# Loading the two halves of an expert weight matrix in one DMA of 2 MB into two neighbouring ring slots

## The reference, cut to what matters

```python
def moe_swiglu(x, w_router, w_gate, w_up, w_down):
    logits = (xt @ w_router).astype(jnp.float32)
    top_val, top_idx = lax.top_k(logits, TOP_K)              # 2 of 8
    top_w = jax.nn.softmax(top_val, axis=-1)
    gates = jnp.sum(jax.nn.one_hot(top_idx, N_EXPERTS) * top_w[..., None], axis=1)
    for e in range(N_EXPERTS):
        y = y + gates[:, e:e + 1] * swiglu(xt, w_gate[e], w_up[e], w_down[e])
```

## Time and profile before

| | us |
|---|---|
| runs | 1366.14, 1364.48, 1365.83 |
| median of the runs | 1365.83 |
| span of the profiled execution, first to last instruction | 1365.5 |
| expert stage, from the profile (first expert gate work to last down) | about 478 to 1350 |

### The profile page before, as it was taken

How to read it: one execution, slowest core, us unless ns; L and a number is a source line. 1 busy time by engine, 2 the same in 40 slices (tenths; PEclk the granted TensorE clock), 3 DMA queues, 4 the chain that set the end, 5 groups by cost and what they waited for, 6 DMA issues and landing times.

```text
span 1365.5 us, 18288 instructions
## 1 busy us (share of the span) xinstructions
PE 1331.8 (98%) x7233; PEld 1123.6 (82%) x7233; DVE 1107.3 (81%) x885; ACT 975.5 (71%) x930; POOL 168.7 (12%) x103
## 2 busy tenths in 40 slices
PE   8989999999999999999999999999999999999996
PEld 7888999999999778777877888777877877787784
DVE  4664655555666599999999989999999999999995
ACT  5465544446556667888788878888888888878883
POOL 4251000000000132574400000000000000000001
PEclk8999999999999999999999999999999999999998
DMA  9305755554542389999999999999999999999992
GB/s 372 121 1 185 207 186 184 184 184 154 204 144 86 111 332 401 404 419 407 412 421 419 421 401 390 422 421 421 408 411 421 414 411 421 421 411 422 418 418 98
DMA packets 67203, 433.24 MB, mean 317 GB/s; under 512 B 8160, under 2 KB 10336, under 8 KB 18992
## 3 DMA queue, kind: packets, MB, share of 16 engines
q1 hardware_dynamic: 60320, 418.01, 76.4%
q0 software_dynamic: 3360, 12.22, 3.0%
q10 hardware_dynamic: 3440, 1.91, 0.8%
HBM read 426.09 MB, written 6.03 MB: 316 GB/s over the span
## 4 chain that ended last, share of the span: by engine, by line
PE 74%; DVE 11%; DMA 9%; ACT 4%; issue 1%; SPq 0%; DVEq 0%; ACTq 0%
PE banks L1887 21%; PE banks L1889 20%; PE banks L1888 20%; DMA raw<-in_moe_w_gate 9%; DVE w_lo L1169 6%; ACT w_hi L623 2%; PE banks L2451 2%; DVE qk_lo L1169 2%; PE banks L2120 2%; PE banks L2452 2%; ACT qk_hi L623 1%; PE banks L2108 1%; PE banks L2488 1%; PE banks L2490 1%; PE banks L2462 1%
## 5 line engine op out<-in xcount | busy, mean ns | idle before, releaser
L1169 DVE TENSOR_TENSOR w_lo<-raw,w_hi 128x2048 fp32r<-128x2048 f32 (+1 forms) x312 | 711.2, 2297 | 134.4 <-ACT w_hi L623 132.9
L623 ACT CAST w_hi<-raw 128x2048 fp32r<-128x2048 f32 (+1 forms) x312 | 592.5, 1909 | 161.8 <-PE banks L1889 125.5
L1169 DVE TENSOR_TENSOR qk_lo<-raw,qk_hi 128x2048 fp32r<-128x2048 f32 x84 | 192.0, 2286 | 13.0 <-ACT qk_hi L623 12.1
L623 ACT CAST qk_hi<-raw 128x2048 fp32r<-128x2048 f32 x84 | 160.0, 1905 | 14.3 <-PE banks L1889 9.5
L1887 PE MATMUL banks<-w_hi,t_hi 128*128 128x512 f32 (+2 forms) x444 | 164.7, 371 | 2.9 <-DVE w_lo L1169 1.5
L1889 PE MATMUL banks<-w_lo,t_hi 128*128 128x512 f32 (+2 forms) x444 | 161.6, 364 | 0.0
L1888 PE MATMUL banks<-w_hi,t_lo 128*128 128x512 f32 (+2 forms) x444 | 161.5, 364 | 0.0
L1887 PE MATMUL banks<-t_hi,w_hi 128*128 128x256 f32 x544 | 155.5, 286 | 0.9 <-DVE t_lo L1190 0.9
L1888 PE MATMUL banks<-t_hi,w_lo 128*128 128x256 f32 x544 | 154.3, 284 | 0.0
L1889 PE MATMUL banks<-t_lo,w_hi 128*128 128x256 f32 x544 | 154.2, 284 | 0.0
L1887 PE MATMUL banks<-w_hi,h_hi 128*128 128x512 f32 x300 | 118.8, 396 | 0.2 <-DVE w_lo L1169 0.2
(11 more groups left out here) (358 smaller groups left out, 2261.9 us busy)
## 6 DMA issues: line engine op xcount, KB each, us to landing
raw<-in_moe_w_gate SPq DMA_DIRECT2D x112, 1024.0 KB, 9.9
raw<-in_moe_w_up SPq DMA_DIRECT2D x112, 1024.0 KB, 9.3
raw<-in_moe_w_down SPq DMA_DIRECT2D x112, 1024.0 KB, 9.7
raw<-in_na_w_qkv SPq DMA_DIRECT2D x12, 1024.0 KB, 4.8
raw<-in_ffn_w_gate SPq DMA_DIRECT2D x11, 1024.0 KB, 5.0
raw<-in_ffn_w_up SPq DMA_DIRECT2D x11, 1024.0 KB, 5.1
raw<-in_ffn_w_down SPq DMA_DIRECT2D x11, 1024.0 KB, 4.9
raw<-in_w_in_e SPq DMA_DIRECT2D x6, 1024.0 KB, 15.7
```

The lines of the kernel that those rows point to most:

```text
L623: act.copy(tile_hi(u, n), raw[:, u.raw, 0:n]).then_inc(hi_done, 1)
L1169: dve.tensor_tensor(tile_lo(u, n), raw[:, u.raw, 0:n], tile_hi(u, n).bitcast(F32), ALU.subtract).then_inc(lo_done, 1)
```

## The change

Gate, up and down of a step are each loaded by one DMA of 2 MB, 16 KB for a partition, into two neighbouring slots. The host lays the weights out so that each partition's 16 KB lie in one piece. The slot numbers of the expert units are shifted by one, so that a pair begins at an even slot. SP waits once for a pair, until VectorE is done with both units that had the two slots; there is one landing semaphore for each pair, and both casts of a pair wait for it. The other weights, the casts, the subtractions and the matmuls are as before.

```diff
     @property
     def raw(self):
-        return self.s % RING
+        return (self.s if self.s < U_MOE else self.s + U_MOE % 2) % RING
...
+    @property
+    def pair(self):
+        return (self.s - U_MOE) // 2 % (RING // 2)
+
     def filled(self):
-        return self.k * 16 + 16 * (self.s // RING + 1)
+        return self.k * 16 + 16 * ((self.s if self.s < U_MOE else self.s - U_MOE) // RING + 1)
...
+        pair_full = [sem(f"pair_full{i}") for i in range(RING // 2)]
...
+            def load_pair(u, src):
+
+                if isinstance(u.k, int) and u.s < U_MOE + RING:
+                    sp.wait_ge(lo_done, min(u.count(-RING + 2), U_MOE))
+                else:
+                    sp.wait_ge(lo_done, u.count(-RING + 1))
+                sp.dma_start(raw[:, u.raw:u.raw + 2, :].rearrange("p r c -> p (r c)"), src).then_inc(pair_full[u.pair], 16)
...
             def gate_up(e, j, base, c):
 
-                for i, w in enumerate((moe_w_gate, moe_w_gate, moe_w_up, moe_w_up)):
-                    load_block(unit_of(base, *c[i]), w[e, j, i % 2])
+                for i, w in enumerate((moe_w_gate, moe_w_up)):
+                    load_pair(unit_of(base, *c[2 * i]), w[e, j])
...
-                    for i, w in enumerate((moe_w_gate, moe_w_gate, moe_w_up, moe_w_up)):
-                        load_block(moe_unit(6 * n - 2 + i), w[expert[v], j, i % 2])
+                    for i, w in enumerate((moe_w_gate, moe_w_up)):
+                        load_pair(moe_unit(6 * n - 2 + 2 * i), w[expert[v], j])
                 v, j = ORDER[n - 1]
-                for i in range(2):
-                    load_block(moe_unit(6 * n + (2 if n < STEPS else -2) + i), moe_w_down[expert[v], j, i])
+                load_pair(moe_unit(6 * n + (2 if n < STEPS else -2)), moe_w_down[expert[v], j])
...
-                act.wait_ge(raw_full[u.raw], u.filled())
+                act.wait_ge(raw_full[u.raw] if u.s < U_MOE else pair_full[u.pair], u.filled())
...
-        by_step = inputs[n].reshape(E, 2, 4, P, MOE_STEPS, HALF).transpose(0, 4, 1, 3, 2, 5)
-        arrays[f"in_{n}"] = np.ascontiguousarray(by_step).reshape(E, MOE_STEPS, 2, P, UNIT)
+        by_step = inputs[n].reshape(E, KD, P, MOE_STEPS, HALF).transpose(0, 3, 2, 1, 4)
+        arrays[f"in_{n}"] = np.ascontiguousarray(by_step).reshape(E, MOE_STEPS, P, 2 * UNIT)
```

More of the change, by code:

```diff
@@ L556, in gate_up @@
             def gate_up(e, j, base, c):
-                for i, w in enumerate((moe_w_gate, moe_w_gate, moe_w_up, moe_w_up)):
-                    load_block(unit_of(base, *c[i]), w[e, j, i % 2])
+                for i, w in enumerate((moe_w_gate, moe_w_up)):
+                    load_pair(unit_of(base, *c[2 * i]), w[e, j])
             def down(e, j, base, c):
-                for i in range(2):
-                    load_block(unit_of(base, *c[i]), moe_w_down[e, j, i])
+                load_pair(unit_of(base, *c[0]), moe_w_down[e, j])
             def middle(e, j, base, sweep):
@@ L2747 @@
     for n in ("moe_w_gate", "moe_w_up"):
-        by_step = inputs[n].reshape(E, 2, 4, P, MOE_STEPS, HALF).transpose(0, 4, 1, 3, 2, 5)
-        arrays[f"in_{n}"] = np.ascontiguousarray(by_step).reshape(E, MOE_STEPS, 2, P, UNIT)
-    by_step = inputs["moe_w_down"].reshape(E, MOE_STEPS, 2, 2, P, D).transpose(0, 1, 2, 4, 3, 5)
-    arrays["in_moe_w_down"] = np.ascontiguousarray(by_step).reshape(E, MOE_STEPS, 2, P, UNIT)
+        by_step = inputs[n].reshape(E, KD, P, MOE_STEPS, HALF).transpose(0, 3, 2, 1, 4)
+        arrays[f"in_{n}"] = np.ascontiguousarray(by_step).reshape(E, MOE_STEPS, P, 2 * UNIT)
+    by_step = inputs["moe_w_down"].reshape(E, MOE_STEPS, 4, P, D).transpose(0, 1, 3, 2, 4)
+    arrays["in_moe_w_down"] = np.ascontiguousarray(by_step).reshape(E, MOE_STEPS, P, 2 * UNIT)
     arrays["in_tables"] = constants()
```

## The result

The changed kernel takes 1462.86 us in the median of 4 runs (1457.79 to 1464.8), the kernel before beside it 1365.99 (4 runs): a ratio of 1.0697, 95% interval 1.0675 to 1.072. The forecast was 1370.8 with a range to 1379. The side was right, the size was short by a factor of nearly twenty, and the side came right by another route than the terms that I added up. The profiled run has a span of 1462.7 us.

A forecast was written before the change was run, and what follows sets the result against it. PE was taken to pace some 13 of 21 expert pairs and the DMA queue the last 8; 2.7 us for unit a's delay plus 2.3 for the queue made 5.0, so 1365.8 became 1370.8 us, range 1362 to 1379.

The forecast's parts named there:

- What bounds the kernel, and the packets: Expert stage: PE sets 13 of 21 pairs' pace, queue (422 GB/s) the last 8; packets fall from 60320 to 36128.
- rival (4): SP's queue: 16 KB rows move as two of 8 KB, 57632 packets, forecast's time; chance inside the forecast's 0.37.
- The rate: Expert loads: half the rows change the time for a MB by at most 0.1 us; taken as 0.
- rival (2): Expert loads: longer rows move faster, 0.05 us a MB gained, giving 1361.4 us; chance 0.15.
- wrong at the root: Sign for the expert stage: the prediction fails if PE's waits do not grow or the queue's rate moves.
- The loop of a slot: Ring slots: a pair's turn takes 13.8 to 14.8 us, under 14.83 and 14.92, so the queue stays full.
- never 12: Sign for gate pairs: landing takes 7.5 to 8.5 us and never reaches 12.
- The delay of unit a: First cast of a pair waits for both units: PE loses 0.45 us in each of six stretches, 2.7 us.
- the queue as the bound: Expert stage: 13 pairs slow from PE's 29.66 us to the queue's 29.84, costing 2.3 us.
- Rival (3): Gate pair's loop is too long, queue runs empty: 0.12 or 0.25 us a step, 1375.8 or 1381 us; chance 0.21.
- Rival (1): The ring absorbs the later landings: no change, cost 1.7 us, 1367.5 us; chance 0.27.
- Entry and end: First pairs and end of the expert stage: cost 0; 2.5 us once if the cover is gone.

The follow-up runs named there:

- m_ring: Ring alone without PE (loads, casts, subtractions), units or pairs, one or both waits: 421 and 422 GB/s with one wait, 379 to 394 with both.
- m_stream: Loads alone, nothing computed, varying DMA size, rows and number in flight: 2 MB with two in flight gave 430 GB/s (16 KB rows) and 423 (8 KB rows).
- m_lead: Loads alone, 2 MB in 16 KB rows, each issue held back 0.2 to 3.4 us by copies on ACT: landings 4.89 to 6.46 us apart.
- m_ring8: Ring alone without PE, 2 MB DMAs, varying slots and columns: 396 GB/s with six slots, 428 with eight, 429 with six and 1536 columns subtracted.
- b_joint_down: Changed kernel with two 1 MB DMAs for a pair, only down pairs awaiting both landings before the first cast: 1436.22 us, ratio 1.0506.

## Why the prediction was wrong

**What bounds the kernel, and the packets**: right. 36128 packets were measured as worked out, so rival (4) is out; the queue's 422 GB/s is what unit loads reach in m_ring too.

**The rate**: I took 0 for longer rows, and rival (2) 0.05 us of 2.485, 2%. m_stream shows 430 against 423 GB/s, so rival (2)'s premise holds, and its conclusion doesn't: the queue is not kept full, and the rate moved to 367, by which I had called myself "wrong at the root". The Trainium skill, DMA: Bandwidth & Descriptors, section Why small descriptors are slow, gives by its cycles for each packet an estimate of 0.6%; the 1.7% measured is more.

**The loop of a slot** is the step that failed: "All are under 14.83, PE's half pair, and 14.92, the queue's, so the queue stays full". The part behind the landing was right: holds of 6.9 (down), 7.1 (up) and 7.4 us (gate), 7.15 on average, where my terms make 6.5, 7.0 and 7.3 to 7.5. The landing was taken as that of an empty queue, 7.3 us, and beside it I asked only whether the sum is under the queue's turn. But a turn of 14.92 us with a hold of 7 leaves a lead of 2 x 4.97 - 7 = 2.9 us, and a queue of 2 MB DMAs lost its rate below a lead of 3.8 to 4.2 (`m_lead`, `m_ring8`). So the landings took 10.3 us, not the 7.5 to 8.5 "never 12" of my sign (the chain has one of 13.67), and the turn came to 10.3 + 7.15 = 17.4 us in place of 14.3. The gate landings of both traces give the sum, from the third step on: 39 turns of a step that took 15.6 us or less before went from 15.0 to 17.0 us on average, 77 us, and the 14 longer ones from 16.8 to 18.2, 19 us. That is 96 of the 97 us. The second part had no term: I had written that in big steps behind big ones the loop "hides". I had the slack fall from 5.8 us to one, and priced that as if the last us were as good as the first.

**The delay of unit a and the queue as the bound**, 5.0 us in sum: the size of what either wait costs alone (7.0 and 5.5 us measured), which may be chance: whether those runs lose it at the places I named isn't shown. In the change itself the two terms are no terms: they assume a queue that keeps its phase.

**Rival (3)** named the place, a pair's loop too long, and its sign came as written, over 30.2 us a pair with a DMA share under 1.00 (34.6 us, 0.96). But it had its price from things put between the casts, 0.12 to 0.25 us a step. `b_joint_down` shows that the loop with nothing between its casts is too long already. Its own prices, 1375.8 and 1381, are nearly as far off as the forecast. I gave it 0.21; with the lead as the quantity to read, it was the likeliest. Rival (1) fell with the 74 us of new PE idle time.

**Entry and end**: the gate pairs of the second to fourth step land 1.2 to 1.4 us earlier than before, so the entry cost nothing. **The clock** stood nowhere in my sum: a late feed is paid again by matmuls at 0.43 us, and PE's busy time in the stage grew by 16 us, up to 13.7 of them by the clock.

No version here that computes the whole reference beats the kernel before. Eight slots were tried in the ring without PE only.

## What to carry to other kernels

A ring's loop has to be checked against the lead, not only against the rate: from the time of a turn take what lies between a landing and the next issue, and see how long before the transfer ahead of it lands the next one is queued. Two waits that each shorten the lead by 2 us were each nearly free here and together set the pace; so price them together. The Trainium skill, SBUF — State Buffer, section The DMA setup-cost knee, says to coalesce into the largest single transfer. This case differs: 1 MB was already fed at 422 GB/s, and the pair in one DMA, with its slots freed and its landing awaited together, cost 7%; of that 6.3 points came with 1 MB DMAs too, by the waits alone.

## What the hardware showed that was not expected

- A queue of 2 MB DMAs kept its rate when the next was issued 4.2 us before the last had landed, and not at 3.8; with issues 1.9 us behind the landing of the DMA two before it moved 367 GB/s and at 3.4 us 338, against 430.
- The DMA engines were busy for 0.96 of the time at 367 GB/s in the changed kernel and for 1.00 of it at 392 in `m_lead`: there most of what is lost lies in packets that take longer, not in empty engines (at 338 GB/s, with a share of 0.89, about half). Most packets still took 0.61 us; the long ones lie largely 1.0 to 2.5 us behind an issue. Why that happens at leads at which no engine is idle, and only after the first few transfers, is open.
- The first sixteen packets of a 2 MB DMA alone on the queue took 0.6 to 2.1 us, those of a full queue 0.61 us (m_stream, m_lead).
- Rows of 16 KB move 1.7% faster than rows of 8 KB in a full queue (430 and 423 GB/s).
- After 3 us in which PE was busy for 0.62 the granted clock of the next 3 was 0.55 and matmuls took 0.43 us, not 0.23, so a stall in the feed costs more than its length.
